# Two layers of a streaming encoder in single-pass fp32: the 640 token columns of each weight tile moved as 512 and 128 instead of 320 and 320

## The reference

```
x += 0.5 * post(down(silu(gate(pre(x))) * up(pre(x))))       half-step FFN 1
P  = pre(x) @ w_in                                            1024 -> 2888 columns
x += post(concat(attention, recurrence, convolution)(P) @ w_out)
x += 0.5 * post(down(silu(gate(pre(x))) * up(pre(x))))       half-step FFN 2
```

## Time and profile before

| | |
|---|---|
| median of 2 runs | 3254.44 us (3252.95 to 3255.93) |
| span of the profiled execution | 3254.3 us |
| PE matmul busy | 2851.5 us, 88% of the span, 18054 matmuls |
| of these the fp32r matmuls of L291 | 2328.3 us, 15648 matmuls |
| PE weight loads busy | 2665.5 us, 82%, 18054 loads |
| DVE, ACT, POOL busy | 1528.1, 944.0 and 476.2 us |
| HBM | 64 GB/s over the span |
| mean granted TensorE clock | 0.937 of 2.4 GHz |

### The profile page before, as it was taken

How to read it: one execution, slowest core, us unless ns; L and a number is a source line. 1 busy time by engine, 2 the same in 40 slices (tenths; PEclk the granted TensorE clock), 3 DMA queues, 4 the chain that set the end, 5 groups by cost and what they waited for, 6 DMA issues and landing times. The chain is left out here.

```text
span 3254.3 us, 44093 instructions
## 1 busy us (share of the span) xinstructions
PE 2851.5 (88%) x18054; PEld 2665.5 (82%) x18054; DVE 1528.1 (47%) x1886; ACT 944.0 (29%) x1237; POOL 476.2 (15%) x328
## 2 busy tenths in 40 slices
PE   1999998997477979999969999989955788999997
PEld 1899998894354879999969999979834458999997
DVE  1633333528965353333353333352499644433333
ACT  1322223216423332212232212231362342322221
POOL 1100001105812120000120000020084313000001
PEclk9999999998768989999989999999976798999998
DMA  5122212113010212122112122122120111212211
GB/s 108 65 71 71 78 63 79 65 52 98 1 73 7 72 52 78 59 83 73 57 60 84 62 81 77 57 73 78 36 76 15 59 46 46 78 68 75 78 61 63
DMA packets 50676, 209.51 MB, mean 64 GB/s; under 512 B 13928, under 2 KB 14312, under 8 KB 34568
## 3 DMA queue, kind: packets, MB, share of 16 engines
q1 hardware_dynamic: 50568, 208.05, 19.3%
HBM read 197.85 MB, written 10.19 MB: 64 GB/s over the span
## 5 line engine op out<-in xcount | busy, mean ns | idle before, releaser
L291 PE MATMUL ps<-hr,wr 128*128 128x320 f32 x11424 | 1707.5, 311 | 83.6 <-DVE hr L407 65.7
L291 PEld LDWEIGHTS ps<-hr,wr 128*128 128x128 f32 x11424 | 1692.3, 189 | 99.7 <-DVE hr L407 43.5
L291 PE MATMUL ps<-hid,wr 128*128 128x320 f32 x4224 | 620.8, 309 | 0.0
L291 PEld LDWEIGHTS ps<-hid,wr 128*128 128x128 f32 x4224 | 619.8, 188 | 0.0
L286 DVE TENSOR_TENSOR wr<-stage,wr 128x2048 fp32r<-128x2048 f32 x184 | 421.7, 2292 | 299.7 <-ACT wr L282 299.7
L282 ACT ACTIVATE wr<-stage 128x2048 fp32r<-128x2048 f32 x184 | 350.6, 1905 | 557.5 <-PE ps L291 288.9
L548 DVE TENSOR_TENSOR arena<-ps,arena 128x640 f32<-128x640 f32 x88 | 72.5, 824 | 545.5 <-PE ps L291 543.8
L523 POOL TENSOR_TENSOR arena<-arena 128x640 f32<-128x640 f32 x28 | 44.3, 1582 | 1737.0 <-ACT arena L499 1737.0
L490 ACT ACTIVATE arena<-arena 128x640 f32<-128x640 f32 x88 | 65.1, 739 | 801.8 <-DVE arena L548 801.8
L860 POOL TENSOR_TENSOR proj<-proj,arena 128x640 f32<-128x640 f32 x120 | 200.1, 1669 | 33.6 <-ACT arena L1018 16.9
L938 PE MATMUL ps<-proj 128*128 128x256 f32 x264 | 90.9, 519 | 97.5 <-issue 78.4
(11 more groups left out here) (204 smaller groups left out, 2224.5 us busy)
## 6 DMA issues: line engine op xcount, KB each, us to landing
stage<-in_wgu SPq DMA_DIRECT2D x88, 1024.0 KB, 4.8
stage<-in_wd SPq DMA_DIRECT2D x32, 768.0 KB, 4.2
stage<-in_w_in SPq DMA_DIRECT2D x24, 1024.0 KB, 4.8
stage<-in_wd SPq DMA_DIRECT2D x32, 640.0 KB, 3.8
stage<-in_w_out SPq DMA_DIRECT2D x8, 1024.0 KB, 5.0
arena<-in_ic SPq DMA_DIRECT2D x16, 256.0 KB, 2.8
hf<-bias_table SPq DMA_DIRECT2D x2, 2048.0 KB, 10.7
arena<-in_kc SPq DMA_DIRECT2D x16, 256.0 KB, 5.2
```

Of the source, the lines that this page charges most:

```text
L291: mm = pe.matmul(out, w(s), v(t), start=start and n == 0, stop=stop and n == 2)
```

## The change

The tokens of a weight tile move in two parts of 512 columns (the prompt) and 128 columns (the samples) in place of two halves of 320. The first part fills a whole bank, the second the first 128 columns of the next one, so the 640 results of a pair of banks lie in one row. `halves` goes, and the readers of PSUM take that row through `bank_pair`. The same holds for the sum of squares in `ones_sum` (plain fp32). The numbers of matmuls, weight loads and other instructions stay as they were on every engine.

```diff
 SEQ, NS, LS, PAST = 512, 8, 16, 512
 TOK = SEQ + NS * LS
 HALF = TOK // 2
+PARTS = ((0, SEQ), (SEQ, TOK))
 KD = D // 128
 KF = DFF // 128
 KA_F, KB_F = 12, KF - 12
...
         def flat(view):
             return view.rearrange("p a n -> p (a n)")
 
-        def halves(view):
-
-            return view.rearrange("p (a n) -> p a n", a=2)
+        def bank_pair(bank):
+
+            return flat(ps[:, bank:bank + 2])[:, 0:TOK]
...
         def product_tile(pe, j, k, c, width, size, v, start, stop):
 
             at_ = k * size + 128 * c
-            for a in range(2):
-                mm = three(pe, ps[:, 4 * j + 2 * c + a, 0:HALF], lambda s: wr[:, j, s, at_:at_ + 128],
-                           lambda t: v[:, t, k, a * HALF:(a + 1) * HALF], start, stop)
+            for a, (lo, hi) in enumerate(PARTS):
+                mm = three(pe, ps[:, 4 * j + 2 * c + a, 0:hi - lo], lambda s: wr[:, j, s, at_:at_ + 128],
+                           lambda t: v[:, t, k, lo:hi], start, stop)
             return mm
...
         def ones_sum(pe, bank, view, done):
 
-            for a in range(2):
-                mm = pe.matmul(ps[:, bank + a, 0:HALF], ones[:], view[:, a * HALF:(a + 1) * HALF],
+            for a, (lo, hi) in enumerate(PARTS):
+                mm = pe.matmul(ps[:, bank + a, 0:hi - lo], ones[:], view[:, lo:hi],
                                start=True, stop=True)
             mm.then_inc(done, 1)
...
                 act.wait_ge(self.total, 1)
-                act.activation(halves(rs), ps[:, 4:6, 0:HALF], ACT.Sqrt, bias=EPS, scale=1.0 / D).then_inc(self.root, 1)
+                act.activation(rs, bank_pair(4), ACT.Sqrt, bias=EPS, scale=1.0 / D).then_inc(self.root, 1)
...
-                                dve.tensor_tensor(halves(sg[:, 0]), ps[:, 4 * j:4 * j + 2, 0:HALF], rs2,
+                                dve.tensor_tensor(sg[:, 0], bank_pair(4 * j), rs2,
                                                   ALU.mult).then_inc(g_scaled, 1)
-                                dve.tensor_tensor(halves(sg[:, 1]), ps[:, 4 * j + 2:4 * j + 4, 0:HALF], rs2,
+                                dve.tensor_tensor(sg[:, 1], bank_pair(4 * j + 2), rs2,
                                                   ALU.mult).then_inc(evac, 1)
...
-                            src = ps[:, 4 * j:4 * j + 2, 0:HALF]
+                            src = bank_pair(4 * j)
                             if f0 == 0:
-                                dve.tensor_copy(halves(yv[:, i, j, :]), src).then_inc(evac, 1)
+                                dve.tensor_copy(yv[:, i, j, :], src).then_inc(evac, 1)
                             else:
-                                dve.tensor_tensor(halves(yv[:, i, j, :]), halves(yv[:, i, j, :]), src,
+                                dve.tensor_tensor(yv[:, i, j, :], yv[:, i, j, :], src,
                                                   ALU.add).then_inc(evac, 1)
...
```

More of the change, by code:

```diff
@@ L538, in _ @@
                     lead.dve_norm(dve)
-                    rs2 = halves(rs)
+                    rs2 = rs
                     if n0 == 0:
@@ L620, in _ @@
                             dve.wait_ge(used, i * 2 + (PROJ + j + 1))
-                            dve.tensor_tensor(halves(pv[:, i, j, 0, :]), ps[:, 4 * j:4 * j + 2, 0:HALF], rs2, ALU.mult)
-                            dve.tensor_tensor(halves(pv[:, i, j, 1, :]), ps[:, 4 * j + 2:4 * j + 4, 0:HALF], rs2,
+                            dve.tensor_tensor(pv[:, i, j, 0, :], bank_pair(4 * j), rs2, ALU.mult)
+                            dve.tensor_tensor(pv[:, i, j, 1, :], bank_pair(4 * j + 2), rs2,
                                               ALU.mult).then_inc(evac, 1)
@@ L625, in _ @@
                     dve.wait_ge(used, OUTP - 1)
-                    dve.tensor_tensor(halves(pv[:, NU // 2 - 1, 0, 0, :]), ps[:, 0:2, 0:HALF], rs2, ALU.mult)
-                    dve.tensor_tensor(halves(pv[:, NU // 2 - 1, 0, 1, :]), ps[:, 2:4, 0:HALF], rs2,
+                    dve.tensor_tensor(pv[:, NU // 2 - 1, 0, 0, :], bank_pair(0), rs2, ALU.mult)
+                    dve.tensor_tensor(pv[:, NU // 2 - 1, 0, 1, :], bank_pair(2), rs2,
                                       ALU.mult).then_inc(evac, 1)
                     dve.wait_ge(used, OUTP)
-                    dve.tensor_tensor(halves(pv[:, NU // 2 - 1, 1, 0, :]), ps[:, 4:6, 0:HALF], rs2,
+                    dve.tensor_tensor(pv[:, NU // 2 - 1, 1, 0, :], bank_pair(4), rs2,
                                       ALU.mult).then_inc(evac, 1)
@@ L691, in _ @@
                         for c in range(2):
-                            cp = dve.tensor_copy(halves(y[:, 2 * s + c]), ps[:, 4 * j + 2 * c:4 * j + 2 * c + 2, 0:HALF])
+                            cp = dve.tensor_copy(y[:, 2 * s + c], bank_pair(4 * j + 2 * c))
                         cp.then_inc(evac, 1)
```

## The result

The changed kernel takes 3627.9 us (median of 2 runs, 3627.74 to 3628.06) against 3254.44 us before, a ratio of 1.114 with a 95% interval of 1.112 to 1.116. The forecast was 3597 us in a range of 3490 to 3870 us. The profiled execution has a span of 3625.3 us.

The account below looks back on a forecast made before the run. PE's fp32r matmuls were taken to bound the kernel. From 3254.3 us, +354 us for 7824 pairs each 45.3 ns longer, less 11 us absorbed by waits in the leads, gave 3597 us, range 3490 to 3870 us.

Parts of the forecast that it names:

- The bound: In eight stages of 2367 us together, PE sets the pace with L291's fp32r matmuls; added matmul cost passes almost in full.
- The short part: The 128-column matmuls: 112 ns each, bound by the next weight load; upper end 125 ns.
- the restart: PE resuming after a wait: the second weight load begins 0.11 us after the first, taken as the load's time.
- The long part: The 512-column matmuls: bound by their columns, 226.7 ns each, with ends of 213 and 235 ns.
- the 13.4 ns over the columns: Time of a 320-column step at full clock (146.7 ns) beyond its columns at 2.4 GHz (133.3 ns).
- What comes back: First pair of tiles in six leads: PE's waits absorb the increase in seven of eight matmul groups, -11 us.
- The reading of PSUM and the rest: One row of 640 read instead of two of 320, and the sum of squares: edits costed at nothing.
- Rival 1: Fp32r matmul pairs: price follows columns alone, short part 67 ns, pair 294 ns, time 3254 us; chance 0.10.
- Rival 2: Fp32r matmul stream: the 147 ns step is the load's own, short part 147 ns, 3758 to 3862 us; chance 0.18.
- Rival 3: Short fp32r matmuls fall to plain fp32's pace, 216 ns each, pair 443 ns, time near 4390 us; chance 0.10.

Follow-up runs that it names:

- the first experiment: Against the kernel before: halves of 320 columns kept, but laid across the bank border so PSUM is read as one row of 640; 3255.26 us, ratio 0.9994.

## Why the prediction was right, and where its sizes were off

**The bound.** PE set the pace: the stretches grew by 371.7 us of 371.0, and nothing outside them moved.

**The short part.** Predicted 112 ns, measured 110.5. Its cause is shown from both sides: half the load brings it to about 60 ns, a quarter of the columns leaves it at 111. The two rows that gave it were a stream with one moving column, whose weights are plain fp32, and the restart, with fp32r weights but a single distance; no row had a short fp32r matmul. That the two agreed carried the step, and it held.

**The long part.** Here the sum was mis-sized: 226.7 ns taken, 232.2 measured. I kept the 13.4 ns over the columns as a fixed surplus. The four lengths now known, 146.8 ns at 320 columns, 174.9 at 384, 203.0 at 448 and 232.2 at 512, lie within 1 ns of a line of 4.5 ns plus 0.4446 ns a column, against 0.4167 at 2.4 GHz. These are means: at 384 and 448 columns single steps of a turn lie up to 7 ns off the line. So most of the surplus grows with the columns, and the value lies nearer to the upper end (235) than to the one I took. With 5.5 ns more on the long part and 1.5 less on the short one, a pair is 4.0 ns over my sum, 7824 x 4.0 = 31 us, which is the distance from 3597 to 3628 to within a few us.

**What comes back.** Predicted -11 us. PE's idle time before these matmuls fell from 83.6 to 74.3 us, 9.3 us; the wait on the lo parts from 65.7 to 57.3.

**The reading of PSUM and the rest.** Costed at nothing, and the first experiment finds nothing.

**Rival 1** (columns alone, no change) falls: a pair costs 342.7 ns, not 294. **Rival 2** (the 147 ns are the load's own) falls: the loads stand 110 ns apart. The surplus spoke for it, and the runs show most of that to grow with the moving columns. **Rival 3** (pace of plain fp32, 216 ns) falls with the same number.

**Still open** is why a column takes 0.4446 ns at full clock when at clock 0.50 the step had nothing over the earlier trace rows. The runs repeat this at every length: at clock 0.50 the middle (median) step is 267, 320, 373 and 427 ns for 320, 384, 448 and 512 columns, which is the columns at 1.2 GHz, and 213 ns for a short part of 128, the load's time at that clock in the earlier trace rows. The loads of the change in its second output projection, at clock 0.50, show steps of 0.43, 0.43 and 0.21 us:

```profile
2961.69 0.33 PEld L292 LDWEIGHTS ps<-hr,wr 128*128 128x128 f32 x1
2962.12 0.33 PEld L292 LDWEIGHTS ps<-hr,wr 128*128 128x128 f32 x1
2962.55 0.33 PEld L292 LDWEIGHTS ps<-hr,wr 128*128 128x128 f32 x1
2962.76 0.33 PEld L292 LDWEIGHTS ps<-hr,wr 128*128 128x128 f32 x1
```

So the prediction's pair at half clock, 427 + 213 = 640 ns, is what was measured, and the surplus shows at full clock alone. Fewer weight columns did not bring it down, and no run here tried the moving side. Open as well are the 1 to 2 ns by which the long parts differ between kernels.

No split tried beats equal halves. At 384 and 256 the short part's columns are by the line still 8 ns over the load, and 0.7% is lost all the same.

## What to carry to other kernels

A matmul stream has two prices for each step, the moving columns and the load of the next weights, and the larger counts; with weights of 128x128 in fp32r the load is 110 ns at full clock, so parts of fewer than some 240 columns pay for columns that they don't move. The 240 are an estimate from the line, (110 - 4.5) / 0.4446, and 256 columns already cost a little here. A split that fills a bank and leaves a short rest saves no matmul and exposes a load for every rest: keep the parts equal, and well above the load. To find the load's price in a trace without such a case, look for a stream with hardly any moving columns, and for the second load after a wait.

## What the runs showed of the hardware that was not expected

- At full clock an fp32r step grows by 0.4446 ns a column, 2.25 columns a nanosecond rather than 2.4, with about 4.5 ns fixed (means, 320 to 512 columns).
- At clock 0.50 that surplus is gone: 320 to 512 columns take 267 to 427 ns, the columns at 1.2 GHz.
- Where the columns are shorter than the load, a step goes by the load beside it and not by the matmul's own weights: 59.5 ns for 128 weight columns beside a load of 64, 108.8 ns for 64 beside a load of 128.
- Where load and columns are close (256 columns, 118 against 110 ns), the step is 122.8 ns on average, over both, in two patterns that change from stage to stage.
- Mixing weight loads of 64 and 128 columns made the kernel with halves 0.8% slower, though a load of 64 has the shorter row (137 against 189 ns).
- A long matmul took 232.2 ns beside short ones of 128 columns and 234.6 ns beside those of 32.
